# High weights in a run, then low weights: regrouping the matmuls of three feed-forward layers

## What is computed

```
def first_block(...):                      # DEPTH = 1, D_FF = 4096
    ...                                    # attention, x = x + merged @ w_out
    h2 = rmsnorm(x, mlp_norm_g)
    x = x + jnp.square(jax.nn.relu(h2 @ w_ff1)) @ w_ff2

def second_block(...):                     # DEPTH_2 = 2, D_FF_2 = 2816
    for layer in range(2):
        h = h + mixer(rms_norm(h, attn_norm[layer]))
        gate, up = jnp.split(rms_norm(h, ffn_norm[layer]) @ w_gu[layer], 2, axis=-1)
        h = h + (jax.nn.silu(gate) * up) @ w_down[layer]
    return rms_norm(h, final_norm)
```

## Time and profile before

| | us |
|---|---|
| median of 3 runs | 960.89 (960.56 to 962.05) |
| the profiled execution | 961.82 |
| its span, first to last instruction | 960.0 |
| PE matmul busy | 938.5 (98%) |
| DVE busy | 736.5 (77%) |
| ACT busy | 545.1 (57%) |
| POOL busy | 102.3 (11%) |

### The profile page before, as it was taken

One profiled execution on the slowest core, in us unless ns is written; L12 is line 12 of the kernel. 1 busy time (PEld: TensorE's weight loads), 2 busy tenths in 40 slices (PEclk: granted clock), 3 DMA queues, 4 the chain that ended last, 5 costly groups with the idle time before them and its releaser, 6 DMA issues.

```text
span 960.0 us, 16452 instructions
## 1 busy us (share of the span) xinstructions
PE 938.5 (98%) x6364; PEld 842.7 (88%) x6364; DVE 736.5 (77%) x1531; ACT 545.1 (57%) x1061; POOL 102.3 (11%) x134
## 2 busy tenths in 40 slices
PE   7989999999999999999999999999999999999997
PEld 7989899988888889889888888899877988888887
DVE  6889855697777675966998888768898589888871
ACT  6667653566555465776644444558687564444452
POOL 3110002300000050003110101210000110100120
PEclk8999999999999999999999999999999999999999
DMA  8977235496454464316945645557311346445621
GB/s 284 239 193 218 88 133 176 152 259 227 158 214 175 175 220 143 121 46 198 272 159 214 220 160 191 203 173 258 113 46 45 136 173 219 177 148 201 220 88 44
DMA packets 25983, 165.12 MB, mean 172 GB/s; under 512 B 3320, under 2 KB 3704, under 8 KB 7472
## 3 DMA queue, kind: packets, MB, share of 16 engines
q1 hardware_dynamic: 23504, 156.09, 46.7%
q0 software_dynamic: 2400, 7.97, 4.4%
HBM read 161.03 MB, written 3.01 MB: 171 GB/s over the span
## 4 chain that ended last, share of the span: by engine, by line
PE 85%; DVE 5%; ACT 4%; DMA 4%; issue 1%; SPq 0%; POOL 0%; DVEq 0%
PE banks L591 22%; PE banks L911 13%; PE banks L594 11%; PE banks L915 8%; PE banks L565 4%; PE banks L569 4%; PE banks L573 4%; DMA scratch<-VR 3%; PE banks L614 3%; PE banks L616 2%; PE banks L618 2%; ACT PN L1462 1%; PE banks L840 1%; PE banks L576 1%; PE banks L577 1%
## 5 line engine op out<-in xcount | busy, mean ns | idle before, releaser
L1777 DVE TENSOR_TENSOR lo<-stage,hi 128x1024 fp32r<-128x1024 f32 x291 | 353.7, 1230 | 19.9 <-ACT hi L1218 18.2
L1218 ACT ACTIVATE hi<-stage 128x1024 fp32r<-128x1024 f32 x291 | 295.9, 1043 | 28.0 <-DMA stage<-in_stream 13.9
L591 PE MATMUL banks<-HT,hi 128*128 128x512 f32 x920 | 232.2, 394 | 0.0
L591 PEld LDWEIGHTS banks<-HT,hi 128*128 128x128 f32 x920 | 165.1, 188 | 33.7
L594 PEld LDWEIGHTS banks<-HT,lo 128*128 128x128 f32 x920 | 125.4, 189 | 9.7
L594 PE MATMUL banks<-HT,lo 128*128 128x256 f32 x920 | 128.0, 282 | 0.0
L2538 POOL TENSOR_TENSOR SQ<-SQ 128x256 f32<-128x256 f32 x40 | 43.4, 1091 | 422.9 <-ACT SQ L1236 421.9
L2276 DVE TENSOR_REDUCE U<-banks 128x256 f32<-128x512 f32 x73 | 50.3, 690 | 29.6 <-PE banks L594 29.2
L911 PE MATMUL banks<-HC,hi 128*128 128x512 f32 x196 | 70.5, 398 | 0.0
L565 PE MATMUL banks<-HT,hi 128*128 128x256 f32 (+3 forms) x348 | 56.3, 297 | 9.7 <-ACT HT L1228 4.9
L915 PE MATMUL banks<-HC,lo 128*128 128x256 f32 x224 | 63.0, 281 | 0.0
(11 more groups left out here) (348 smaller groups left out, 1785.8 us busy)
## 6 DMA issues: line engine op xcount, KB each, us to landing
stage<-in_stream SPq DMA_DIRECT2D x144, 1024.0 KB, 4.9
BT<-scratch POOLq DMA_DIRECT2D x8, 256.0 KB, 15.9
BT<-scratch POOLq DMA_DIRECT2D x4, 512.0 KB, 17.4
stage<-in_stream SPq DMA_DIRECT2D x3, 512.0 KB, 9.7
scratch<-VR POOLq DMA_DIRECT2D x2, 768.0 KB, 21.3
XT<-in_xt SPq DMA_DIRECT2D x4, 256.0 KB, 6.5
B<-scratch POOLq DMA_DIRECT2D x4, 256.0 KB, 6.4
out<-ROWS SPq DMA_DIRECT2D x4, 256.0 KB, 2.5
```

The source lines that it names most:

```text
L591: e.matmul(out[:, 0:512], hi[:, j % HI_SLOTS, 128 * k:128 * k + 128], HT[:, :, k, :], start=k == 0, stop=False)
L1218: e.activation(hi[:, j % HI_SLOTS, 0:w], stage[:, j // 2 % ST_PAIRS, j % 2, 0:w], ACT.Copy).then_inc(*up("hi", ("hi", j, 0)))
L1777: e.tensor_tensor(lo[x], stage[x], f32(hi[:, j % HI_SLOTS, 0:sched[j][2]]), ALU.subtract).then_inc(*up("lo", ("lo", j, 0)))
```

## The change

Three things change, none of them in what is computed.

1. **Blocks of a down projection in groups by weights.** Behind the wide tiles, a `_down` slab is now used in one go: eight 512s (two hidden tiles by four banks), then eight 256s. So are the `_rest` slabs: all 512s of one output tile in the slab, then its 256s. "First four" runs its eight 512s and then two 256s for each bank. `_down_behind` says behind which tile a `_down` slab is used: in "ff" slab f/2 - 2 behind even f from 4 on and slab 14 behind f = 31; in the other two slab f//2 - 1 behind odd f from 3 on (slabs counted from 0).
2. **Two wide tiles together.** `wide_features` takes two slabs (two "ff1" tiles, or "gate" and "up" of one f): sixteen 512s into two banks, then eight 256s into the first, which releases the first slab, and eight into the second.
3. **Squares.** In the stages "swa" and "nsa" GpSimd adds squares 1 to 6, VectorE adds square 7 to that sum, and TensorE multiplies one sum with ones, not two.

The order of the slabs in the stream follows the order of use.

```diff
+def _down_behind(kind, f):
+    if kind == "ff":
+        return 14 if f == 31 else f // 2 - 2 if f >= 4 and f % 2 == 0 else None
+    return f // 2 - 1 if f >= 3 and f % 2 else None
...
-        def wide_features(out, j, rows, done):
-            for k in range(8):
+        def wide_features(js, rows):
+            for j in js:
+                clear(where[j])
                 q.wait_ge(*at("hi", j, 0))
-                q.wait_ge(*at("high", rows.name, k))
-                q.wait_ge(*at("low", rows.name, k))
-                e.matmul(out[:, 0:512], hi[...], HT[:, :, k, :], start=k == 0, stop=False)
-            for k in range(8):
+                for k in range(8):
+                    q.wait_ge(*at("high", rows.name, k))
+                    q.wait_ge(*at("low", rows.name, k))
+                    e.matmul(bank[where[j]][:, 0:512], hi[...], HT[:, :, k, :], start=k == 0, stop=False)
+            for j in js:
                 q.wait_ge(*at("lo", j, 0))
-                last = e.matmul(out[:, 0:256], lo[...], rows.high(k), start=False, stop=k == 7)
-            last.then_inc(*up("tile", *done))
+                for k in range(8):
+                    last = e.matmul(bank[where[j]][:, 0:256], lo[...], rows.high(k), start=False, stop=k == 7)
+                last.then_inc(*up("tile", ("slab", j)))
+                free[where[j]] = [("halves", j)]
...
-                if f >= 2:
-                    d = f - 2
-                    if d % 2 == 0:
-                        now[0] = take(kind + "_down", d // 2)
-                    for c in range(4):
-                        if d == 0:
-                            clear(c)
-                        high_block(kind, now[0], 4 * (d % 2) + c, c, d, d == 0)
-                        x = low_block(kind, now[0], 4 * (d % 2) + c, c, d, False)
-                    if d % 2:
-                        x.then_inc(*up("tile", ("slab", now[0])))
+                    now.append(take(kind + "_" + u, f))
+                    where[now[-1]] = next_bank()
+                    if len(now) == 2 or f == n - 1 and u == ups[-1]:
+                        wide_features(now, rows)
+                        now = []
+                i = _down_behind(kind, f)
+                if i is not None:
+                    j = take(kind + "_down", i)
+                    for d in (2 * i, 2 * i + 1):
+                        for c in range(4):
+                            if d == 0:
+                                clear(c)
+                            high_block(kind, j, 4 * (d % 2) + c, c, d, d == 0)
+                    for d in (2 * i, 2 * i + 1):
+                        for c in range(4):
+                            x = low_block(kind, j, 4 * (d % 2) + c, c, d, False)
+                    x.then_inc(*up("tile", ("slab", j)))
...
                 if what == "first four":
                     j = take(kind + "_down", n // 2 - 1)
+                    for d in (n - 2, n - 1):
+                        for c in range(4):
+                            high_block(kind, j, 4 * (d % 2) + c, c, d, False)
                     for c in range(4):
                         for d in (n - 2, n - 1):
-                            high_block(kind, j, 4 * (d % 2) + c, c, d, False)
                             y = low_block(kind, j, 4 * (d % 2) + c, c, d, d == n - 1)
...
                     if c < 3:
-                        high_block(kind, j, o, b, f, f == 0)
-                        y = low_block(kind, j, o, b, f, f == n - 1)
+                        for i in range(end - f):
+                            high_block(kind, j, o + i, b, f + i, f + i == 0)
+                        for i in range(end - f):
+                            y = low_block(kind, j, o + i, b, f + i, f + i == n - 1)
...
         def last_squares(sq, stage, c):
             q.wait_ge(*at("square", stage, c, 7))
+            if last_of_sums(stage) == 6:
+                q.wait_ge(*at("squares so far", stage, c, 6))
+                e.tensor_tensor(first, first, b, ALU.add).then_inc(*up("sums_dve", ("squares", stage, c, 0)))
...
         def root_first(b, stage, which):
             clear(b)
-            squares_by_rows(bank[b], stage, which, 2)
+            squares_by_rows(bank[b], stage, which, 1)
```

More of the change, by code:

```diff
@@ L41, in _mlp_order @@
         s += [(kind + "_" + u, f, 1024) for u in ups]
-        if f >= 2 and f % 2 == 0:
-            s.append((kind + "_down", (f - 2) // 2, 1024))
+        d = _down_behind(kind, f)
+        if d is not None:
+            s.append((kind + "_down", d, 1024))
     first = (n - 3) // 8 + 1
@@ L507, in square_place, with last_of_sums @@
         return k if sq is SQ or k == 0 else 1 + (k + 1) % 2
+    def last_of_sums(stage):
+        return 6 if stage in ("swa", "nsa") else 5
     def rest_steps(kind, n):
         for c in range(4):
-            for f in range(n):
+            f = 0
+            while f < n:
                 i, o = divmod(c * n + f, 8)
@@ L517, in rest_steps @@
                     yield "take", i
-                yield "block", (c, f, o)
-                if f == n - 1:
+                end = min(f + 8 - o, n if f >= n - 2 or c else n - 2)
+                yield "blocks", (c, f, end, o)
+                if end == n:
                     yield "tile", c
-                if o == 7:
+                if o + end - f == 8:
                     yield "give", i
+                f = end
     def out_tile(name, p):
@@ L655, in squares_by_rows @@
                     for t in range(2):
-                        m = e.matmul(out[:, 2 * c + t:2 * c + t + 1], sq[:, square_place(sq, (0, 6, 7)[i]), 128 * t:128 * t + 128], ones[:, 0:1], start=n == 0, stop=n == last)
+                        m = e.matmul(out[:, 2 * c + t:2 * c + t + 1], sq[:, square_place(sq, (0, 6, 7)[i]) if parts > 1 else 0, 128 * t:128 * t + 128], ones[:, 0:1], start=n == 0, stop=n == last)
                         if n == last:
@@ L964, in feed_forward @@
                     js[x] = take(kind + "_rest", x)
-                elif what == "block":
-                    c, f, o = x
+                elif what == "blocks":
+                    c, f, end, o = x
                     b, j = sum_bank(stage, 4 + c), js[(c * n + f) // 8]
@@ L970, in feed_forward @@
                     if c < 3:
-                        high_block(kind, j, o, b, f, f == 0)
-                        y = low_block(kind, j, o, b, f, f == n - 1)
-                    else:
-                        y = narrow_block(kind, j, o, b, f, f == 0, f == n - 1)
-                    done = [("slab", j)] * (o == 7) + [("sum", stage, 4 + c)] * (f == n - 1)
+                        for i in range(end - f):
+                            high_block(kind, j, o + i, b, f + i, f + i == 0)
+                        for i in range(end - f):
+                            y = low_block(kind, j, o + i, b, f + i, f + i == n - 1)
+                    else:
+                        for i in range(end - f):
+                            y = narrow_block(kind, j, o + i, b, f + i, f + i == 0, f + i == n - 1)
+                    done = [("slab", j)] * (o + end - f == 8) + [("sum", stage, 4 + c)] * (end == n)
                     if done:
@@ L1533, in feed_forward @@
                 activate(f)
-                if f >= 2 and f % 2 == 0:
-                    j = slabs.take(kind + "_down", (f - 2) // 2)
-                elif f >= 2:
-                    slabs.give(j)
+                if _down_behind(kind, f) is not None:
+                    slabs.give(slabs.take(kind + "_down", _down_behind(kind, f)))
                 slabs.high_parts(3)
@@ L1786, in last_squares @@
             q.wait_ge(*at("square", stage, c, 7))
-            a, b = (sq[:, square_place(sq, k), :] for k in (6, 7))
-            e.tensor_tensor(a, a, b, ALU.add).then_inc(*up("sums_dve", ("squares", stage, c, 1)))
+            first, a, b = (sq[:, square_place(sq, k), :] for k in (0, 6, 7))
+            if last_of_sums(stage) == 6:
+                q.wait_ge(*at("squares so far", stage, c, 6))
+                e.tensor_tensor(first, first, b, ALU.add).then_inc(*up("sums_dve", ("squares", stage, c, 0)))
+            else:
+                e.tensor_tensor(a, a, b, ALU.add).then_inc(*up("sums_dve", ("squares", stage, c, 1)))
         def add_bank(b, sums, stage, bias=None):
@@ L2537, in add_square @@
             q.wait_ge(*at("square", stage, c, k))
-            e.tensor_tensor(sq[:, 0, :], sq[:, 0, :], sq[:, square_place(sq, k), :], ALU.add).then_inc(*up("sums", ("squares so far", stage, c, k), *[("squares", stage, c, 0)] * (k == 5)))
+            e.tensor_tensor(sq[:, 0, :], sq[:, 0, :], sq[:, square_place(sq, k), :], ALU.add).then_inc(*up("sums", ("squares so far", stage, c, k), *[("squares", stage, c, 0)] * (k == 5 and stage not in ("swa", "nsa"))))
         def sum_squares(stage, both=False):
```

16 lines of the change are left out of this document (6 added, 10 removed).

## The result

The changed kernel takes 955.43 us (median of 6 runs, 954.68 to 955.81), the kernel before beside it 961.47 (6 runs, 959.24 to 962.40): ratio 0.994, 95% interval 0.9928 to 0.9951. So it is 6.0 us faster by these medians, 5.5 against the 960.89 of the first three runs. The forecast was 955.6.

What follows compares the result with a forecast made beforehand. PE, busy 98% of the span, was taken as the bound by its pace. Grouping 4.1 + squares 1.2 = 5.3 us less: profiled 961.82 to 956.5, median 960.89 to 955.6; range 952.2 to 959.0.

Steps and rivals of the forecast that it cites:

- What bounds: Whole kernel: PE, busy 98% of the span, is the bound, in the feed-forwards by its own pace and not by waits.
- Grouping, 4.1: Three feed-forwards: 1452 regrouped pairs take 506.7 us against 510.8, 4.1 less, with 133 changes at 0.025 us each.
- an alternation spoils what is behind it: Feed-forwards: a wide tile behind alternating blocks takes 0.04 us over its floor, behind another wide tile 0.02 to 0.03.
- The settling: PE's stream: alternating widths never settle, 0.0066 us per pair over the floor; runs do, losing mainly where 256s change to 512s.
- Squares, 1.2: Attention stages "swa" and "nsa": half the squares' rows go, 0.85 and 0.4 us; 1.2 taken, between nothing and 1.25.
- all of it moves forward: "swa": the root's row still waits 0.36 us for DVE, but its whole chain starts earlier by what the squares save.
- The covers costed at nothing: Feed-forwards: earlier high weights (2.4 us of cover at slab 51) and "first four" bank reuse (0.5 us) cost nothing.
- 1 (changing stays dear): Feed-forwards: each of 133 changes costs 0.04 us or runs never settle; 957.6 to 958.7 us in all; chance 0.18.
- 2 (pace by columns alone): Feed-forwards: order of widths is worth nothing, only the squares' 1.2 us is gained; 959.7 us; chance 0.07.
- 3 (no cost): Feed-forwards: changing widths costs nothing, grouping brings 7.4 us and squares 1.25; 952.2 us; chance 0.07.
- 4 (DVE late): SwiGLU feed-forwards: DVE takes the bound, an f takes 7.3 us against 7.02; about 970 us in all; chance 0.08.
- Signs: PE's trace: sixteen 512s in 3.65 us, eight-pair block groups 2.80, first feed-forward at most 165.0, second at most 170.5.

Runs made afterwards that it cites:

- third experiment: The changed kernel with 512s and 256s of the down-projection blocks in turn again, wide tiles still two together; 956.70 us, ratio 0.9958 to the kernel before.
- fourth: The changed kernel with wide tiles run one by one, blocks still in groups; 955.91 us, ratio 0.9947 to the kernel before.
- seventh experiment: The third experiment with four thrown-away transposes ahead of the first block of outputs 4, 5 and 6 of each feed-forward; 961.92 us in one run.

## Why the prediction was right

- **What bounds: right.** PE by its pace, in 98% of the span before and after; what PE's stream lost, the time lost.
- **Grouping, 4.1: right in mechanism, measured 4.62.** I counted the third feed-forward as the second, 172.1, but it took 173.21; with that, before was 511.92 in sum, not 510.8. The third holds twelve transposes, eight ahead of output 6 (0.79 us from start to start) and four ahead of the narrow output (0.35), which both kernels pay, so this error does not touch the difference. The price of a change was 0.0194, not 0.025: 8 x (349.1 - 346.7) for the blocks, 16 x (347.9 - 346.7) for the wide tiles. 133 of these are 2.6. With the floor, 503.4, and the transposes, 1.15, that is 507.1; measured 507.30. The 0.2 left stands at the first wide 512 of the first feed-forward, which takes 0.42 to the next instead of 0.23, before as after. The sum had this stall in what it measured before and not in what it worked out for after; that hides a part of the 0.7 by which it overrated the changes, so its 4.1 owes a little to luck.
- **Where the gain comes from.** The blocks no longer in turn are worth 1.63 (third experiment), two wide tiles together 1.14 (fourth). These sum to 2.77, less than the 4.62. What is left, 1.85, is in neither, since both experiments keep a third thing: a `_down` slab is used in one go, so that eight blocks and not four stand between wide tiles. No run has this alone, but the rows give it a price. The wide tile behind four pairs in turn cost 352.0 per pair before (every wide tile of the first feed-forward, the first of each f in the others; the second there 349.1). Wide groups behind eight pairs in turn cost 346.8, in the others 347.3; behind a group of blocks 347.9. My estimate for slabs in one go, with blocks in turn and wide tiles one by one, takes 346.9 for a tile behind eight pairs in turn and 353.9 for these eight (third experiment), and 349.1 for a tile behind a tile. In the first feed-forward 24 pairs would cost 8 x 346.9 + 8 x 349.1 + 8 x 353.9 ns = 8.399 us. Before, they cost 16 x 352.0 + 8 x 353.2 ns = 8.458, and there are 14 such stretches. In the others 40 pairs would cost 8 x 346.9 + 24 x 349.1 + 8 x 353.9 ns = 13.985 us against 32 x 350.6 + 8 x 352.6 ns = 14.040, in about 19 stretches. That is 1.9 us, all of what is left, but no run shows it by itself. The prediction's reading that an alternation spoils what is behind it was half right: four pairs did, eight did not.
- **The settling: right for long runs, wrong as a law.** "In a run it does, and what is lost is lost mainly where 256s change to 512s" fits eight and sixteen. Runs of two (348.3) refute a fixed price per change: at 0.0194 for every two pairs a pair would cost 356. "With the kinds in turn PE never settles" is refuted by the earlier trace rows and what follows them: from 937.24 on, output 6 stays at 346.7 to its end. The prediction took five pairs of it as a sign that the loss is a state that the order can also miss, and that was right. What selects the state is open; four transposes ahead do not (seventh experiment). For this output the grouping is a small loss: with its dear first pair it cost 350.8 per pair before and 353.0 after the change, 0.05 us over 22 pairs.
- **Squares, 1.2: measured 1.07** (0.78 and 0.29 for 0.85 and 0.4), confirmed from both sides. The wait of 0.36 stays, as the step said. But "all of it moves forward" did not hold. The rows themselves gave 0.89 and 0.45; about 0.1 came back in "swa" at the later wait for ZR (1.02 before, 1.15 after), and 0.14 in "nsa", where the root's row now begins 0.06 us behind the end of DVE's root. The prediction had named such a loss only as the lower bound of its range.
- **The covers costed at nothing: right.** Slab 51 is split by 195.1 (ACT) and wanted at 195.91 + 1.84 = 197.75 in the trace after, 2.6 us of cover where 2.4 were worked out. No wait of PE is shown in the feed-forwards. At "first four" DVE makes tile 0's two additions from 331.29 and 331.75, done at 332.17, and PE takes the freed bank for output 5 at 332.50: 0.3 us of cover where 0.5 were worked out. In the span's remainder only the attentions' waits are left.
- **Rivals.** 1 (changing stays dear) is out: 0.019 and not 0.04. 2 (pace by columns alone) is out: with the same instructions at clock 1.00 the order alone moved 353.3 to 348.3. By that reading every order of the same pairs would take the same time. The formula of the Trainium skill ("TensorE: Matmul & The Clock Gate", section "Back-to-back issue gap"), with nothing in it but the columns, says the same, and the traces disagree. The prediction left out that this section gives the formula for an isolated matmul, and about 131 ns per matmul of 512 columns for a sustained stream. No 512 in the feed-forwards here has less than 224 ns to the next start, so that figure does not fit either. 3 (no cost) is out: 507.3 and not 503.4. 4 (DVE late) is out: of DVE's 2.41 idle per two f, 1.93 are a wait for PE, and no wait of PE is shown there.
- **Signs.** The sixteen 512s took 3.66 (3.65 named), the block group 2.79 (2.80), the first feed-forward 164.69 (165.0 or less), the root's wait 0.36. One was missed: the second feed-forward took 170.69, and I had named 170.5 or less. That bound was set tighter than the sum allowed: 490 x 0.3467 + 44 x 0.025 is 171.0, and with the measured 0.0194 it is 170.7.

The head start of 1.40 in the profiled execution belongs to none of the steps. A start that varies so makes the single times of the block variants (953.65 to 955.73) useless for ranking what differs by 0.5 us: the fastest, runs of three, owes 0.7 of its lead over after to its head. By stages runs of two in the blocks are best, 0.46 under the change, in one run; that is below what the whole time can tell here, so I claim no better version.

## What to carry to other kernels

Where TensorE is the bound and no wait shows, look at the distances between starts by neighbour: here 512s and 256s in turn cost 353.3 ns per pair against 348.3 to 350.7 in groups, about 1%, and groups of two already gave it, while equal widths in turn cost no more than a run. It is no law for every place: in one output pairs in turn ran at 346.7, cheaper than the blocks of any group here. Count also what stands behind an alternation, and how long it is: by the estimate above that was the largest of the three parts. Such a regrouping is worth doing only where buffers allow it without making another engine late, and its gain is worked out as pairs by difference, not from busy time. Compare variants stage by stage in the trace: here that tells some 0.03 us, where the intervals of the whole time are about 2 us wide.

## What the runs showed of the hardware that I had not expected

- The cost in ns of a pair of mixed widths is not monotone in the length of a run: 353.3 in turn, 348.3 in twos, 349.6 in threes, 350.7 in fours, 349.1 in eights.
- It depends on width and not on which weights are loaded: 226.7 ns per 512 with high and low weights in turn.
- Pairs in turn have two steady paces, 353.3 and 346.7, the second in output 6 of the third feed-forward in three kernels. What selects the state stays open: behind eight transposes it was the fast one, behind four and behind twelve the slow one.
- The pace of a run depends on where the pattern before it stopped: a wide tile behind four pairs in turn 352.0, a wide tile or group behind eight 346.8. By starts, pairs in turn repeat every three, and the next run's first 512 takes the distance that comes next in the pattern, 241 behind four and 236 behind eight. Whether their number or the place in the pattern decides, no run separates.
- The first 190 us vary by 2.8 us between executions, and the stages behind them, where their instructions are the same, by 0.03 us at most.
